# Spreading the norm sums and bias transposes among the modulation rows, and sharing the first scaling between VectorE and ScalarE

## The chip, the cores and the metric

The kernel runs on one NeuronCore of a Trainium2 chip. The metric is the device time of one execution in microseconds (us), lower is better; the figure for the kernel before is the median of three runs. Everything is float32.

## The reference, cut to what matters

The program computes two transformer blocks over 256 tokens of width 1024. The first is a conditioned block (attention of two kinds over 256 latent and 256 context tokens, then a mixture of 32 experts), the second has four mixers and a gated feed-forward. The change touches only the start of the first block:

```python
mod_lat = (jax.nn.silu(c) @ w_ada[l] + b_ada[l])[:, None, :]
mod_ctx = (jax.nn.silu(c_ctx) @ w_ada[l] + b_ada[l])[None, None, :]
sa, sca, ga, sf, scf, gf = jnp.split(mod_lat, 6, axis=-1)
...
def rmsnorm(x, w):
    xf = x.astype(jnp.float32)
    y = xf * lax.rsqrt(jnp.mean(xf * xf, axis=-1, keepdims=True) + EPS)
    return (y * w.astype(jnp.float32)).astype(x.dtype)

def modulate(h, shift, scale):
    return h * (1 + scale) + shift

l_dq, l_dk, ... = mixer_inputs(modulate(rmsnorm(x, attn_norm_w[l]), sa, sca), *mp, ang)
c_dq, c_dk, ... = mixer_inputs(modulate(rmsnorm(ctx, attn_norm_w[l]), csa, csca), *mp, None)
```

`mixer_inputs` multiplies these activations by `w_in` (the projections dq, dk, cq, ckv, kr, dv), rotates some of them (rope) and normalises others.

## The kernel before, in words

**Layout and order.** Activations are held transposed, features on the 128 partitions in 8 tiles k = 0 to 7, tokens along the free axis. `hT[:, k, 256:512]` holds tile k of the latent activations, `hT[:, k, 0:256]` that of the context. The order of the whole first part is one hand-written list, `PRE` (from L324): a list of steps, over which each engine loops by itself (`tensor_pre`, `vector_pre`, `scalar_pre`) and emits its own share of each step, so that a step's place in the list is its place in every engine's queue. GpSimd has its own program (`pool_pre`).

**The modulation row.** `w_ada` comes in 8 loads of 1 MB per third of it, one for each k. Step `("mrow", 0, k)` (L555) multiplies the padded silu of the two conditions by load k, in four column groups that accumulate in one PSUM bank. After the eighth, ScalarE copies the bank out (L830), `("mcol", 0)` transposes it with four matmuls (L562), VectorE adds the bias (L1025) and makes `aw = (1 + scale) * weight` in two instructions (L1035, L1037).

**The first norm.** ScalarE squares x (L867) into `hT[:, k, 0:256]`; steps `("xsum", 0)` and `("xsum", 4)` add the squares over the partitions by multiplying with ones (L581, four tiles each). ScalarE takes the root (L874), VectorE the reciprocal (L1028) and eight products `x * r` (L1032). Then `("h", 0)` multiplies each of the eight tiles by its column of `aw` and adds the shift, in place (L1043, eight VectorE instructions). Each raises `h_ready`, on which the matmuls of dq wait, tile by tile (L595).

**Bias transposes.** Steps `("b1t", 0..3)` transpose the experts' biases (L539), with a ScalarE copy each (L819); nothing needs them before the experts.

**The context.** `("ctxsquare",)` has ScalarE square the context (L854); `("rms", "ctx")` sums these (L588, after the second dq), and `("h", 1)` scales the context's tiles, VectorE first (L1047), ScalarE after (L879). From dk on the matmuls need both halves: they wait for `h_ready` of 8 + k + 1.

**Loads.** SyncE issues all big loads in one queue: x, the eight `w_ada` loads, then w_in for dq (two), the context, and the rest of w_in; a load into a slot waits until the matmuls that used the slot are done (L1782). The second third of `w_ada` is not multiplied by TensorE but added up by VectorE, `("add", k)` (L1019, L1016), beside the projections.

**GpSimd's tables.** `pool_pre` builds four tables one after the other by doubling (L759 to L767, from 4 elements a partition up to 512), writes each to DRAM with two DMAs (L773, L774) and waits for these before it starts the next (the memset at L749). The last instruction of a table raises `table_done`.

**The attention's start.** In `PRE`, after the projections, come two steps `score` (scores of one head and token tile; VectorE takes the maxima, L1098, ScalarE the exponentials, L924), then `("soft", 0, 0)` (VectorE, L1108 to L1117), qn, qr, a third score, and then qn, qr, kn (L633) and mv (L638), whose results ScalarE and VectorE move out of PSUM (qn at L901). VectorE's share of every `soft` begins with

```python
                elif kind == "soft":
                    w.wait_ge(table_done, 4)
```

Dense groups from there on rotate over four PSUM banks: the first kn (`("kn", 0)`) takes the bank of `("qn", 1)` and so waits for ScalarE's copy of that one, which stands in ScalarE's queue behind the exponentials of the third score, and these wait for VectorE's maxima, which stand behind `("soft", 0, 0)` in VectorE's queue.

After the attention come the output projection, the router, and the experts in the order of how many tokens they have; their weights (384 MB in all) stream in through SyncE's queue. The second block follows.

Of the kernel before, what the change touches and what calls it, by code (L numbers as in the profile page):

```python
# [5 lines left out]
ALU = mybir.AluOpType  # L6
ACT = mybir.ActivationFunctionType
# [170 lines left out]
def build(nc, I, out):  # L178
    ctx = ExitStack()
    with ctx:  # L180
# [3 lines left out]
        def sem(name):  # L184
            return ctx.enter_context(nc.semaphore(name))
# [20 lines left out]
        def Pm(name, i=None):  # L206
            a, b = PAR[name]
            return par[:, a:b] if i is None else par[:, a + i:a + i + 1]
# [32 lines left out]
        b1t = arena[:, TOP:AR]  # L241
# [3 lines left out]
        xv = xT[:, :].rearrange("p (k t) -> p k t", k=8)  # L245
# [6 lines left out]
        ctx_in, x_in, more_in = sem("ctx_in"), sem("x_in"), sem("more_of_cst_in")  # L252
        silu_e, c2_zero, c2_ready = sem("silu_e"), sem("c2_zero"), sem("c2_ready")
        sq_ready, sq_spent, rb_ready = sem("sq_ready"), sem("sq_spent"), sem("rb_ready")
        h_scaled, h_ready, rope_done, rope_kept = sem("h_scaled"), sem("h_ready"), sem("rope_done"), sem("rope_kept")
        norm_ready, lam_sem = sem("norm_ready"), sem("lam_ready")
        max_ready, p_ready = sem("max_ready"), sem("p_ready")
# [33 lines left out]
        rbs = take(2, 256)  # L291
        ctxT = take(8, 256)
        hT = take(8, 512)
# [15 lines left out]
        mods = sm(96).rearrange("p (j v) -> p j v", v=2)  # L309
        aw = sm(16).rearrange("p (j v) -> p j v", v=2)  # L310
# [11 lines left out]
        w_in = I["w_in"]  # L322

        PRE = [("silu",)] + [("phase", i) for i in range(8)] + [("power", k) for k in range(7)] + [("rms", "x")]  # L324
        PRE += [("mrow", 0, k) for k in range(4)] + [("xsum", 0), ("mrow", 0, 4), ("xsum", 4), ("mrow", 0, 5), ("b1t", 0), ("mrow", 0, 6), ("b1t", 1), ("mrow", 0, 7)]
        PRE += [("mcol", 0), ("b1t", 2), ("b1t", 3), ("aw",), ("h", 0), ("ctxsquare",)]
        late = []

        BESIDE = {("dk", j): [("add", j)] for j in range(4)}
# [43 lines left out]
        for i in range(len(UNITS) + 1):  # L373
# [10 lines left out]
            if i and i % 2 == 0:  # L384
                h = i // 2 - 1
# [28 lines left out]
        for s in PRE:  # L414
            kind = s[0]
            if kind == "mrow":
                m, k = s[1:]
# [7 lines left out]
            elif kind == "add":  # L425
                k = s[1]
# [94 lines left out]
        def tensor_pre(pe, w):  # L521
# [10 lines left out]
            for s in PRE:  # L532
                kind = s[0]
                if kind == "b1t":
# [3 lines left out]
                    for j in range(4):  # L538
                        i = pe.transpose(psum(s, j * 128, (j + 1) * 128)[0:32, :], b1col[:, :, s[1] * 4 + j], ident)  # L539
                    i.then_inc(pe_done, 1)  # L540
                elif kind == "mrow":
                    m, k = s[1:]
# [13 lines left out]
                elif kind == "mcol":  # L556
# [4 lines left out]
                    for j in range(4):  # L561
                        i = pe.transpose(psum(s, j * 128, (j + 1) * 128), rowb[m % 2][:, j * 128:(j + 1) * 128], ident)  # L562
                    i.then_inc(pe_done, 1)
                elif kind == "subroot":
                    room(G[s])
                    for h in range(4):
                        w.wait_ge(sub_square, h + 1)
                        i = pe.matmul(psum(s, 0, 256)[32 * h:32 * h + 32, :], ones[:, 0:32], sqh[h], start=True, stop=True, skip_group_check=True)
                    i.then_inc(pe_done, 1)
                elif kind == "subln":  # L570
                    h = s[1]
# [10 lines left out]
                elif kind == "rms" and s[1] != "x":  # L582
# [3 lines left out]
                    for k in range(K):  # L586
                        w.wait_ge(sq_ready, q + k + 1)
                        i = pe.matmul(psum(s, 0, n), ones, hT[:, k, 0:256] if s[1] == "ctx" else sqb[(q + k) % 2][:, 0:n], start=k == 0, stop=k == K - 1, skip_group_check=True)  # L588
                        i.then_inc(sq_spent, 1)
                elif kind in ("dq", "cq"):  # L590
                    j = s[1]
                    room(G[s])
                    for k in range(8):
                        w.wait_ge(h_ready, k + 1)
                        i = pe.matmul(psum(s, 0, 256), tile("w_" + kind, k, j * 128, (j + 1) * 128), hT[:, k, 256:512], start=k == 0, stop=k == 7, skip_group_check=True)  # L595
                    i.then_inc(pe_done, 1)
                elif kind in ("dk", "ckv"):
                    room(G[s])
                    key, a = ("w_dk", s[-1] * 128) if kind == "dk" else ("w_cq", 256)
                    for k in range(8):  # L600
                        w.wait_ge(h_ready, 8 + k + 1)
                        i = pe.matmul(psum(s), tile(key, k, a, a + 128), hT[:, k, :], start=k == 0, stop=k == 7, skip_group_check=True)
                    i.then_inc(pe_done, 1)
                elif kind == "kr":
                    room(G[s])
                    for k in range(8):
                        w.wait_ge(h_ready, 8 + k + 1)
                        for q in range(2):
                            i = pe.matmul(psum(s)[64 * q:64 * q + 64, :], tile("w_cq", k, 384, 448), hT[:, k, :], start=k == 0, stop=k == 7, skip_group_check=True)
                    i.then_inc(pe_done, 1)  # L610
# [6 lines left out]
                elif kind in ("qn", "qr"):  # L617
                    h = s[1]
# [10 lines left out]
                elif kind == "kn":  # L629
                    h = s[1]  # L630
# [19 lines left out]
                elif kind == "score":  # L650
                    _, h, t = s
# [25 lines left out]
                elif kind == "value":  # L677
                    h = s[1]
# [106 lines left out]
        def scalar_pre(act, w):  # L785
# [4 lines left out]
            for s in PRE:  # L790
# [64 lines left out]
                elif kind == "rms":  # L855
# [16 lines left out]
                    w.wait_ge(eps_set, 1)  # L872
                    w.wait_ge(sq_spent, q + K)
                    act.activation(rms_into(key), psum(s, 0, n), ACT.Sqrt, scale=1.0 / RMS_D[key], bias=eps).then_inc(moved[g.bank], 1)  # L874
                elif kind == "h" and s[1]:
                    w.wait_ge(moved[G["mcol", 0].bank], G["mcol", 0].use)
                    for k in range(8):
                        w.wait_ge(h_scaled, k + 1)
# [54 lines left out]
        def vector_pre(dve, w, own):  # L933
            dt, th, kk, wc, wsn, lbr, lbi, dn, t1, t2, t3, t4, t5 = phase_t
            are, aim = Pm("s5_are"), Pm("s5_aim")
            for s in PRE:
# [89 lines left out]
                elif kind == "rms":  # L1026
                    w.wait_ge(moved[g.bank], g.use)
                    dve.reciprocal(rms_into(s[1]), rms_into(s[1])).then_inc(rb_ready, 1)  # L1028
                    if s[1] == "x":
                        w.wait_ge(rb_ready, T["rb", "x"])  # L1030
                        for k in range(8):
                            own.count(dve.tensor_tensor(hT[:, k, 256:512], xv[:, k, :], rbs[:, 0, :], ALU.mult))  # L1032
                elif kind == "aw":
                    w.wait_ge(moved[G["mcol", 0].bank], G["mcol", 0].use)
                    own.count(dve.tensor_scalar(aw, mods[:, 8:16, :], 1.0, None, ALU.add))  # L1035
                    own.wait()
                    own.count(dve.tensor_tensor(aw, aw, Pm("attn_w").unsqueeze(2).to_broadcast([128, 8, 2]), ALU.mult))  # L1037
                    own.wait()
                elif kind == "h":
                    if s[1] == 0:  # L1040
                        own.wait()
                        for k in range(8):
                            dve.tensor_scalar(hT[:, k, 256:512], hT[:, k, 256:512], aw[:, k, 0:1], mods[:, k, 0:1], ALU.mult, ALU.add).then_inc(h_ready, 1)  # L1043
                        continue
                    w.wait_ge(rb_ready, T["rb", "ctx"])
# [2049 lines left out]
```

## Time and profile before

| | |
|---|---|
| median of three runs | 1820.44 us (1818.83 to 1822.33) |
| the profiled execution | 1820.19 us |
| its span in the trace | 1818.1 us |
| TensorE busy | 1654.9 us, 91% of the span |
| VectorE busy | 480.2 us, 26% |
| ScalarE busy | 263.0 us, 14% |
| GpSimd busy | 145.7 us, 8% |
| read from HBM | 540.33 MB |

Start times in the rows are microseconds from the start of the span. PE is TensorE's matmuls, DVE is VectorE, ACT ScalarE, POOL GpSimd. In a row of the timeline "[6.16 <-issue]" says how long the engine sat idle before the row and what ended that; PEclk is the granted clock of TensorE as a share of 2.4 GHz, so 0.50 is 1.2 GHz. A float32 matmul of the program shows up as two records.

### The profile page before, as it was taken

The page shows a single profiled execution, that of the slowest core. Times are in us where ns is not written, and L with a number is a line of the kernel's source. Part 1 is how long each engine was busy: PE and PEld are TensorE (multiplying, and loading weights), DVE is VectorE, ACT ScalarE, POOL GpSimd, SP SyncE. Part 2 cuts the span into 40 slices and gives each one's busy share as a digit, 9 for nine tenths or more (in the row PEclk, how much of TensorE's full clock was granted, in tenths as well). Part 3 has the DMA queues.
Part 4 walks back from the last instruction along what each step waited for, and adds up shares of the span by engine and source line. Part 5 has one row for each costly group of instructions (what it writes and reads, how often), then busy time and mean ns, then how long its engine had stood idle before and what let it go on. Part 6 is the DMA issues. An engine that isn't in the chain of part 4 may idle for free.

```text
span 1818.1 us, 19674 instructions
## 1 busy us (share of the span) xinstructions
PE 1654.9 (91%) x8178; PEld 1004.8 (55%) x8178; DVE 480.2 (26%) x1012; ACT 263.0 (14%) x554; POOL 145.7 (8%) x277
## 2 busy tenths in 40 slices
PE   5999999949997699948899996899999999999997
PEld 2644674414343154413344442377778888888886
DVE  5656421202121102202111220245576212211101
ACT  2114321101011011101011110023213100200000
POOL 6673000000000000000000000010002000000000
PEclk8999999979998799978999998999999999999998
DMA  9567478999999999999999999963452344534340
GB/s 375 204 234 263 168 306 349 428 419 424 425 426 428 426 428 424 424 428 427 421 427 426 427 427 427 419 242 120 158 180 99 134 144 162 209 118 160 139 162 24
DMA packets 93916, 546.95 MB, mean 301 GB/s; under 512 B 6539, under 2 KB 18455, under 8 KB 62844
## 3 DMA queue, kind: packets, MB, share of 16 engines
q1 hardware_dynamic: 88960, 529.82, 72.0%
q0 software_dynamic: 4128, 14.42, 2.2%
q8 instruction: 67, 1.10, 0.2%
q10 hardware_dynamic: 732, 1.38, 0.2%
q14 instruction: 29, 0.24, 0.0%
HBM read 540.33 MB, written 7.62 MB: 301 GB/s over the span
## 4 chain that ended last, share of the span: by engine, by line
PE 64%; DMA 20%; DVE 1%; SPq 1%; issue 0%; ACT 0%; DVEq 0%
PE PS L1408 16%; DMA arena<-in_w 11%; DMA ring<-in_w 9%; PE PS L2368 8%; PE PS L1433 8%; PE PS L2202 4%; PE PS L2394 4%; PE PS L2215 3%; PE PS L2223 3%; PE PS L1384 2%; PE PS L1444 2%; PE PS L2209 2%; PE PS L1418 2%; PE PS L2358 2%; PE PS L2231 2%; PE PS L2249 1%
## 5 line engine op out<-in xcount | busy, mean ns | idle before, releaser
L1408 PE MATMUL PS<-arena 128*64 128x512 f32 (+2 forms) x984 | 271.2, 651 | 60.1 <-DMA ring<-in_w 39.7
L1408 PE MATMUL PS<-ring,arena 128*64 128x512 f32 (+2 forms) x928 | 220.7, 636 | 41.8 <-DMA arena<-in_w 29.0
L1408 PEld LDWEIGHTS PS<-arena 128*64 128x64 f32 (+2 forms) x984 | 84.1, 139 | 201.1 <-issue 200.5
L1433 PE MATMUL PS<-ring,arena 128*64 128x512 f32 (+2 forms) x576 | 143.2, 628 | 11.4 <-DMA ring<-in_w 7.2
L2368 PE MATMUL PS<-arena,ring 128*128 128x256 f32 x704 | 152.5, 379 | 0.0
L1680 DVE TENSOR_SCALAR arena<-PS 128x512 f32<-128x512 f32 x28 | 19.4, 691 | 501.7 <-PE PS L1418 501.7
L1408 PEld LDWEIGHTS PS<-ring,arena 128*64 128x64 f32 (+2 forms) x928 | 67.1, 134 | 152.0 <-issue 151.5
L2368 PEld LDWEIGHTS PS<-arena,ring 128*128 128x128 f32 x704 | 133.6, 190 | 18.1
L1433 PE MATMUL PS<-arena 128*32 128x512 f32 (+2 forms) x392 | 96.1, 619 | 8.7 <-DMA ring<-in_w 5.0
L1433 PEld LDWEIGHTS PS<-ring,arena 128*64 128x64 f32 (+2 forms) x576 | 46.4, 138 | 88.1 <-issue 88.1
L2202 PE MATMUL PS<-arena,ring 128*128 128x256 f32 x384 | 85.0, 380 | 0.7 <-DVE arena L2673 0.7
L1545 ACT ACTIVATE arena<-arena 128x512 f32<-128x512 f32 x28 | 17.5, 630 | 424.2 <-DVE arena L1680 424.2
L2202 PEld LDWEIGHTS PS<-arena,ring 128*128 128x128 f32 x384 | 72.2, 190 | 11.7 <-issue 1.3
L2833 POOL DMA_DIRECT2D arena<-in_s_bre x1 | 0.6, 611 | 944.3 <-DVE xT L1714 944.3
L2394 PE MATMUL PS<-arena,ring 128*128 128x256 f32 x352 | 76.1, 379 | 0.0
L2394 PEld LDWEIGHTS PS<-arena,ring 128*128 128x128 f32 x352 | 66.9, 190 | 9.1
L1433 PEld LDWEIGHTS PS<-arena 128*32 128x32 f32 (+2 forms) x392 | 29.5, 128 | 60.0 <-issue 59.1
L1408 PE MATMUL PS<-cst,arena 128*32 128x512 f32 (+2 forms) x136 | 61.1, 592 | 0.0
L1384 PEld LDWEIGHTS PS<-arena 128*128 128x128 f32 x448 | 54.1, 196 | 10.0 <-issue 9.6
L2215 PE MATMUL PS<-arena,ring 128*128 128x256 f32 x256 | 58.4, 382 | 0.0
L1694 DVE COPY arena<-PS 128x512 f32<-128x512 f32 x14 | 9.7, 692 | 183.8 <-PE PS L1433 183.8
L2223 PE MATMUL PS<-arena,ring 128*128 128x256 f32 x256 | 58.0, 379 | 0.0
(479 smaller groups left out, 2051.5 us busy)
## 6 DMA issues: line engine op xcount, KB each, us to landing
ring<-in_w SPq DMA_DIRECT2D x92, 2048.0 KB, 22.1
arena<-in_w SPq DMA_DIRECT2D x74, 2048.0 KB, 22.9
ring<-in_w_ada SPq DMA_DIRECT2D x24, 1024.0 KB, 8.6
arena<-in_w SPq DMA_DIRECT2D x24, 1024.0 KB, 20.2
cst<-in_w SPq DMA_DIRECT2D x24, 1024.0 KB, 20.7
ring<-in_w_in SPq DMA_DIRECT2D x22, 1024.0 KB, 13.7
ring<-in_w_up SPq DMA_DIRECT2D x20, 1024.0 KB, 8.7
ring<-in_w_gate SPq DMA_DIRECT2D x16, 1024.0 KB, 7.0
```

What stands on the lines that cost most here:

```text
L1384: m = pe.matmul(bank(("gx", i, c), j * S, (j + 1) * S), of[:, j % 2, :], sel[:, t, :], start=t == 0, stop=t == 1, skip_group_check=True)
L1408: m = pe.matmul(bank(("up", i, b))[rows[n], :], xs[:, k, rows[n]], tiles[n][:, b * 512:(b + 1) * 512], start=k == 0, stop=False, skip_grou ...
L1418: m = pe.matmul(bank(("up", i, b))[rows[n], :], one.to_broadcast([128, width]), b1t[:, b * 512:(b + 1) * 512], start=False, stop=True, ski ...
L1433: m = pe.matmul(bank(("down", i, c))[rows[n], :], actT[:, k, rows[n]], tiles[n][:, a:a + 512], start=k == 0, stop=k == 7, skip_group_check ...
L1444: m = pe.matmul(bank(("y", i, c), q * 256, (q + 1) * 256), ysr[:, j * 128:(j + 1) * 128], pgt[i % 3], start=True, stop=True, skip_group_ch ...
L2202: i = pe.matmul(psum(s, q * 256, (q + 1) * 256), tile((name, j // 4), k, a, a + 128), xn[:, k, :], start=k == 0, stop=k == 7, skip_group_c ...
L2209: i = pe.matmul(psum(s, 0, m), xn[:, k, t * 128:(t + 1) * 128], tile((name, j), k, 0, m), start=k == 0, stop=k == 7, skip_group_check=True)
L2215: i = pe.matmul(psum(s, 0, 256), tile(("wgate", bi, f // 4), k, f % 4 * 128, f % 4 * 128 + 128), xn[:, k, :], start=k == 0, stop=k == 7, s ...
L2223: pe.matmul(psum(s, 0, 256), tile(("wgate", bi, f // 4), k, a, a + 128), xn[:, k, :], start=k == 0, stop=k == 7, skip_group_check=True)
L2231: i = pe.matmul(psum(s, 256, 512), tile(("wbr", bi, f // 4), k, a, a + 128), yt[:, k, :], start=k == 0, stop=k == K - 1, skip_group_check= ...
L2368: return pe.matmul(psum(("ff", f), half * 256, half * 256 + 256), tile((key, f // 4), k, a, a + 128), src[:, k, :], start=k == 0, stop=k = ...
L2394: i = pe.matmul(psum(("acc", j // 2), j % 2 * 256, j % 2 * 256 + 256), tile(("wd", c), k % 2, j * 128, (j + 1) * 128), hh[:, k, :], start= ...
```

## The change

It has three parts.

1. **The order of `PRE`.** The two xsum steps stand after the second and the third modulation row (they stood after the fourth and the fifth), and the four b1t steps after the fourth to the seventh row (they stood after the sixth and the seventh, and two of them behind `mcol`).
2. **The products `x * r`.** VectorE makes those of the even tiles first, then those of the odd ones; the odd ones raise a semaphore of their own, `x_scaled`.
3. **The step `("h", 0)`.** VectorE scales the four even tiles; ScalarE scales the four odd ones with an Identity activation whose scale and bias are columns of `aw` and of the modulation (raising `h_other`). The waits of dq, cq, dk, ckv and kr are renumbered to match. ScalarE's new share stands in its queue between the copies of the modulation row and the squares of the context.

```diff
         PRE = [("silu",)] + [("phase", i) for i in range(8)] + [("power", k) for k in range(7)] + [("rms", "x")]
-        PRE += [("mrow", 0, k) for k in range(4)] + [("xsum", 0), ("mrow", 0, 4), ("xsum", 4), ("mrow", 0, 5), ("b1t", 0), ("mrow", 0, 6), ("b1t", 1), ("mrow", 0, 7)]
-        PRE += [("mcol", 0), ("b1t", 2), ("b1t", 3), ("aw",), ("h", 0), ("ctxsquare",)]
+        PRE += [("mrow", 0, 0), ("mrow", 0, 1), ("xsum", 0), ("mrow", 0, 2), ("xsum", 4), ("mrow", 0, 3), ("b1t", 0), ("mrow", 0, 4), ("b1t", 1)]
+        PRE += [("mrow", 0, 5), ("b1t", 2), ("mrow", 0, 6), ("b1t", 3), ("mrow", 0, 7), ("mcol", 0), ("aw",), ("h", 0), ("ctxsquare",)]
...
                     for k in range(8):
-                        w.wait_ge(h_ready, k + 1)
+                        w.wait_ge(h_other if k % 2 else h_ready, k // 2 + 1)
                         i = pe.matmul(psum(s, 0, 256), tile("w_" + kind, k, j * 128, (j + 1) * 128), hT[:, k, 256:512], start=k == 0, stop=k == 7, skip_group_check=True)
...
-                        w.wait_ge(h_ready, 8 + k + 1)
+                        w.wait_ge(h_ready, 4 + k + 1)
...
-                elif kind == "h" and s[1]:
+                elif kind == "h" and not s[1]:
+                    w.wait_ge(aw_ready, 1)
+                    for k in range(1, 8, 2):
+                        w.wait_ge(x_scaled, k // 2 + 1)
+                        act.activation(hT[:, k, 256:512], hT[:, k, 256:512], ACT.Identity, scale=aw[:, k, 0:1], bias=mods[:, k, 0:1]).then_inc(h_other, 1)
+                elif kind == "h":
...
                         w.wait_ge(rb_ready, T["rb", "x"])
-                        for k in range(8):
-                            own.count(dve.tensor_tensor(hT[:, k, 256:512], xv[:, k, :], rbs[:, 0, :], ALU.mult))
+                        for k in (0, 2, 4, 6, 1, 3, 5, 7):
+                            i = dve.tensor_tensor(hT[:, k, 256:512], xv[:, k, :], rbs[:, 0, :], ALU.mult)
+                            if k % 2:
+                                i.then_inc(x_scaled, 1)
+                            else:
+                                own.count(i)
                 elif kind == "aw":
                     w.wait_ge(moved[G["mcol", 0].bank], G["mcol", 0].use)
                     own.count(dve.tensor_scalar(aw, mods[:, 8:16, :], 1.0, None, ALU.add))
                     own.wait()
-                    own.count(dve.tensor_tensor(aw, aw, Pm("attn_w").unsqueeze(2).to_broadcast([128, 8, 2]), ALU.mult))
-                    own.wait()
+                    dve.tensor_tensor(aw, aw, Pm("attn_w").unsqueeze(2).to_broadcast([128, 8, 2]), ALU.mult).then_inc(aw_ready, 1)
+                    w.wait_ge(aw_ready, 1)
                 elif kind == "h":
                     if s[1] == 0:
                         own.wait()
-                        for k in range(8):
+                        for k in range(0, 8, 2):
                             dve.tensor_scalar(hT[:, k, 256:512], hT[:, k, 256:512], aw[:, k, 0:1], mods[:, k, 0:1], ALU.mult, ALU.add).then_inc(h_ready, 1)
```

## Rows read from the trace of the kernel before

**Rows 1.** Stretches of 20 us: busy time of each engine, PEclk, DMA share, GB/s
```profile
300.00:320.00 20.00, 20.00 (x98) 7.15 (x96) 4.37 (x8) 3.93 (x7) 0.00 (x0) 1.00 0.64 254
320.00:340.00 20.00, 20.00 (x96) 6.74 (x94) 5.26 (x8) 1.26 (x2) 0.00 (x0) 1.00 1.01 429
```

**Rows 2.** The chain that ended last: start, length, what
```profile
347.48 23.34 DMA arena<-in_w
```

**Rows 3.** TensorE's timeline, 12 to 60 us: start, length, what
```profile
12.78 1.73 PE L555 MATMUL PS<-ring,arena 128*32 128x512 f32 x8 [0.46 <-DMA ring<-in_w_ada]
...
17.76 1.93 PE L555 MATMUL PS<-ring,arena 128*32 128x512 f32 x8 [1.42 <-DMA ring<-in_w_ada]
19.62 2.66 PE L581 MATMUL PS<-arena,cst 128*128 128x256 f32 x8
...
23.21 1.99 PE L581 MATMUL PS<-arena,cst 128*128 128x256 f32 x8
...
28.23 1.06 PE L555 MATMUL PS<-ring,arena 128*32 128x512 f32 x8
30.09 0.66 PE L562 MATMUL PS<-cst,arena 128*128 128x128 f32 x4 [0.80 <-ACT arena L830]
...
37.78 11.13 PE L595 MATMUL PS<-arena,ring 128*128 128x256 f32 x32 [6.16 <-issue]
...
52.19 7.07 PE L595 MATMUL PS<-arena,ring 128*128 128x256 f32 x32
```

**Rows 4.** Timeline of VectorE and ScalarE, 25 to 41 us
```profile
25.29 1.28 ACT L874 ACT_TABLE_LOAD   x1 [13.14 <-PE PS L581]
...
28.88 6.38 DVE L1032 TENSOR_TENSOR arena<-xT,arena 128x256 f32<-128x256 f32 x8
...
36.43 6.05 DVE L1043 TENSOR_SCALAR arena<-arena,small 128x256 f32<-128x256 f32 x8
...
38.23 2.56 ACT L854 ACTIVATE arena<-arena 128x256 f32<-128x256 f32 x8 [5.94 <-DMA arena<-in_ctxT]
```

**Rows 5.** Stretches of 1 us, columns as in rows 1
```profile
34.00:35.00 1.00, 0.00 (x0) 0.00 (x0) 1.00 (x2) 0.00 (x0) 1.00 (x2) 0.83 1.11 353
...
45.00:46.00 1.00, 1.00 (x7) 0.87 (x6) 0.10 (x1) 0.38 (x1) 0.00 (x0) 1.00 1.08 396
```

**Rows 6.** GpSimd's timeline: where the tables end (L773) and start (L749)
```profile
50.12 0.10 POOL L749 MEMSET arena<- 128x4 f32 x1 [7.44 <-DMA phase_scratch<-arena]
...
78.58 0.60 POOL L773 DMA_DIRECT2D phase_scratch<-arena  x1 [0.30 <-POOL arena L767]
...
86.18 0.10 POOL L749 MEMSET arena<- 128x4 f32 x1 [6.47 <-DMA phase_scratch<-arena]
...
119.40 0.60 POOL L773 DMA_DIRECT2D phase_scratch<-arena  x1 [0.30 <-POOL arena L767]
...
125.62 0.10 POOL L749 MEMSET arena<- 128x4 f32 x1 [5.09 <-DMA phase_scratch<-arena]
...
147.97 0.60 POOL L773 DMA_DIRECT2D phase_scratch<-arena  x1 [0.30 <-POOL arena L767]
```

**Rows 7.** Timelines of VectorE, ScalarE and TensorE, 149 to 158 us
```profile
149.02 0.15 DVE L1108 RECIPROCAL small<-small 128x1 f32<-128x1 f32 x1
...
152.78 0.65 ACT L901 ACTIVATE arena<-PS 128x256 f32<-128x256 f32 x2
...
153.80 3.60 PE L633 MATMUL PS<-arena,ring 128*128 128x512 f32 x8
```

**Rows 8.** VectorE's additions, and one table instruction of GpSimd beside and without one
```profile
69.16 3.12 DVE L1016 SCALAR_TENSOR_TENSOR ring<-ring,arena 128x2048 f32<-128x2048 f32 x1
...
106.60 5.43 DVE L1016 SCALAR_TENSOR_TENSOR ring<-ring,arena 128x2048 f32<-128x2048 f32 x2
...
70.09 3.08 POOL L760 TENSOR_TENSOR arena<-arena 128x512 f32<-128x512 f32 x1
...
141.82 1.04 POOL L760 TENSOR_TENSOR arena<-arena 128x512 f32<-128x512 f32 x1
```

More of the change, by code:

```diff
@@ L254, in build @@
         sq_ready, sq_spent, rb_ready = sem("sq_ready"), sem("sq_spent"), sem("rb_ready")
+        aw_ready, h_other, x_scaled = sem("aw_ready"), sem("h_other"), sem("x_scaled")
         h_scaled, h_ready, rope_done, rope_kept = sem("h_scaled"), sem("h_ready"), sem("rope_done"), sem("rope_kept")
@@ L606, in tensor_pre @@
                     for k in range(8):
-                        w.wait_ge(h_ready, 8 + k + 1)
+                        w.wait_ge(h_ready, 4 + k + 1)
                         for q in range(2):
```

## The prediction

> **What bounds the kernel now.** I first read the busy time by stretches, to see whether the start of the program matters to its end. Up to 320 us TensorE is busy all the time while the DMA engines have room (0.64 of their time between 300 and 320 us), and from 320 us on they are full [rows 1]; the chain that ended last turns from TensorE to the experts' loads at 347 us [rows 2]. Those loads start when TensorE frees their space, so what TensorE gains before 320 us, and keeps, comes out at the end one for one; what is regained before that point is worth nothing. Next I read TensorE's timeline of the first 60 us, where it still has holes. The modulation rows run as their loads land (each waits for a DMA); the eighth runs at 28.23, and its transposes end at 30.75 [rows 3]. Then TensorE waits for the first scaled tile until 37.78, and the 32 records of the first two dq take 11.13 us where the next 32 take 7.07 [rows 3]. VectorE's timeline says why: root at 25.29, reciprocal, eight products up to 35.26, then the modulation's bias and `aw`, which were ready to be made since 30.8, then eight scalings from 36.43 to 42.48 [rows 4]. The clock is the second reason: granted full until TensorE had been idle for about 3 us, it falls in the stretch at 34 us and is back at 45 us [rows 5]. Last I followed the path forward from there for a wait that doesn't move with TensorE, and found GpSimd's: its fourth table ends 0.30 us before the DMA at 147.97, at 147.67 [rows 6], and the first soft step, which needs it, starts at 149.02 [rows 7]. That is 1.35 us of slack.
>
> **The front, step by step.** The loads of `w_ada` are not moved, so row eight stays at 28.23 and the transposes at 30.09 to 30.75 [rows 3]. The two b1t steps that stood behind them lie elsewhere now, in waits for loads: nothing gained or lost. The first xsum can start at the end of row two, 12.78 + 1.73 = 14.5; with two xsum steps of 2.66 and 1.99 us and a row between them of 1.06 to 1.93 us the second one ends between 20.2 and 21.1 (before: 25.2) [rows 3]. From there root and table load take 1.80 us (25.29 to the reciprocal at 27.09), the reciprocal 1.79 (to 28.88) and the products 6.38 [rows 4]; so they end at about 30.6 instead of 35.26. The transposes are done at 30.75, so the chain over the norm and the chain over the modulation now end together. From the end of the products to the first scaling it was 36.43 - 35.26 = 1.17 us [rows 4], so scaling starts at 31.9. VectorE's four take 4 x 0.76 = 3.0 us (6.05 / 8 each) [rows 4]; ScalarE's four, by the context's squares of the same size, 4 x 0.32 = 1.3 us (2.56 / 8) [rows 4], beside them. For a scale that is a column, the trace has no ScalarE row on this tile; the bound above is VectorE's 0.76, which would change nothing, since each engine then still keeps the other's pace. The first tile is there at 32.7 and the last at 34.9, instead of 37.2 and 42.5.
>
> At the full clock dq 0 is done 0.44 us behind the last tile (7.07 / 16 for a tile's two records), at 35.4, and dq 1 3.5 us later, at 38.9. At the half clock throughout it would be 32.7 + 14.1 = 46.8. TensorE is idle for only 2 us (30.75 to 32.7), but lightly loaded since 29, and before it kept the full clock for about 3 us of idleness [rows 3, 5]; I take a fall for part of the time, and 41 for the end of dq 1 (39 to 44). The context then has to be there: its squares can't start before 38.23, when its load lands, and take 2.56 us [rows 4], so it costs nothing unless the clock stays full. The sums over the context follow in 3.5 us, and the third dq starts at 44.5 instead of 52.19 [rows 3]: 7.7 us earlier, between 5 and 9.5.
>
> ScalarE's new share stands ahead of the context's squares, and ends at about 33.5 while these wait for a load until 38.23: free, with 4.7 us of cover. The later w_in loads, the additions and the ropes follow TensorE or land ahead of their use. The cst load moves a little; nothing waits for it.
>
> **What becomes of it.** GpSimd's tables hang on its own queue and its own DMAs [rows 6]; they don't move with TensorE. TensorE reaches `("kn", 0)` at 153.80 - 7.7 = 146.1, but that needs the bank of `("qn", 1)`, whose copy ended 4.14 us after soft began (152.78 + 0.38 against 149.02) [rows 7]; and soft can't begin before the table at 147.67 + 0.05. So kn 0 starts at 147.7 + 4.25 = 151.95 at the earliest: of the 7.7 us 1.85 are left (the slack of 1.35, and 0.5 that TensorE had over ScalarE's copy), and TensorE stands still for some 6 us instead.
>
> The table's own end moves, though. A VectorE addition over 2048 elements with two operands in SBUF stops GpSimd for its length: L760 took 3.08 us beside one and 1.04 without [rows 8], 2.0 us lost. The seven of them run between 69.16 and 112.0 [rows 8]; tables two and three took 28.5 and 33.2 us (50.12 to 78.58, 86.18 to 119.40), the fourth, alone, 22.35 [rows 6]. That is 6.1 and 10.9 us over. One of the seven fell at the end of table two and into the DMA wait behind it (78.58 to 86.18), where it cost nothing. The additions now come 5 to 8 us earlier and the tables at most 1; one more of the additions may fall into that wait (2 us gained), the eight products of the context's scaling fall before table two (some 0.9 gained), or the one that was free falls inside table two (2 us lost). I take the fourth table 2 us earlier, with the ends -4 and +2. kn 0 then starts at 149.95, 3.85 us earlier than before.
>
> **The clock at the new stall.** TensorE comes back after some 4 us of idleness, longer than the 3 us after which it had lost its clock at 34 us; from 37.78 it took until 45 to have it again [rows 3, 5]. At half clock for 4 us, half of the work done in them is lost: 2 us (0 if the clock holds, 3.5 if it takes the 7.2 us of before). The Trainium skill (TensorE: Matmul & The Clock Gate, The HAM clock gate) says that an idle stretch puts the array back to 1.2 GHz and that the phase of this gate is not tied to the kernel's start, so that the loss differs from run to run; by that rule the full loss would come in some runs and none in others. The trace agrees as far as one execution can: 0.83 in the stretch at 34 us, behind 2.4 us of idleness [rows 3, 5].
>
> **Sum.** 1820.19 - 1.85 - 2 + 2 = 1818.3 for an execution like the profiled one, which stands 0.25 us under the median of the runs. I predict 1818.3, a gain of some 2 us. The measurement tells about 0.2% (3.6 us) from no change, so this counts as within it.
>
> **Rivals.**
> (A) The tables end earlier still, or the clock holds: 1.85 + 2 to 4, with a loss of 0 to 1, so 4 to 6 us: 1815.2. For it: how many additions fall into the DMA waits is a matter of 2 us each. Against it: a stall over 3 us speaks for a fallen clock. 0.25.
> (B) The gain of the front comes through whole: 1820.2 - 7.7 = 1812.5. It would need the soft step not to wait for the table, or the tables to follow TensorE; the wait stands in the code, and the rows show 1.35 us of slack. 0.04.
> (C) Slower: the additions, moved against the tables, all cost their 2 us, so the fourth table ends 2 us or more later (past 149.5, from where no gain is left: 1.85 - 2), and the clock falls at the stall and takes 7 us to return: 1.85 - 2 - 3.5 = -3.65 and beyond: 1824. For it: only one addition of seven had been free. Against: the context's products leave table two. The Trainium skill (SBUF — State Buffer, Who interferes with whom) has the side that starts second blocked for the other's whole instruction; with the row's 3.12 us instead of my 2.0 for the lost time this rival would be at 1825. 0.08.
> (D) The front gives little, because the clock is low through both dq (third dq at 50.3, 1.9 us earlier): then the table hardly binds, TensorE doesn't stall, and 1818.3 to 1820 comes out as well. 0.10.
>
> **Numbers.** The forecast (table binds, clock falls) has 0.53 and gives 1816.7 to 1820.5. The range, 1814.2 to 1822.5, takes in A and D, half of the clock's and the table's bad ends, and the spread of runs (1.8 us to either side). Faster by over 0.2%: most of A, B, and a tail of the forecast, 0.31. Slower: C, 0.08. The rest, 0.61.
>
> **What would show it.** The products L1032 should start at about 24 and end by 31; four L1043 from about 32, four ScalarE scalings beside them; the third dq at 44 to 46. A wait of VectorE of several us on GpSimd ahead of L1108, about 146 us; a hole of 3 to 6 us on TensorE before L633, and half clock behind it. If the third dq is 7 us earlier and L633 is too, the table is not what I take it for; if L633 starts later than 152, the tables moved the wrong way; if the first dq starts after 35, the front is wrong.

## The result, and the profile after

The change made the kernel slower: 1824.72 us (median of 20 runs, 1822.18 to 1827.91) against 1820.82 (20 runs, 1818.13 to 1825.61), ratio 1.0019 with a 95% interval of 1.0012 to 1.0026. The forecast was 1818.3, no measurable change, with 1814.2 to 1822.5 as its range; the time lies 2.2 us above the range. In time it is rival (C), slower at 1824, that came; its two effects show below (a table that ends later, a clock that falls), but not the cause that it gave for the table. The profiled execution took 1827.03 us, at the slow end of its runs, with a span of 1824.9.

TensorE's timeline of the changed kernel, lines that answer to [rows 3]:

```profile
14.73 2.68 PE L582 MATMUL PS<-arena,cst 128*128 128x256 f32 x8
...
18.33 1.99 PE L582 MATMUL PS<-arena,cst 128*128 128x256 f32 x8
...
28.05 1.06 PE L556 MATMUL PS<-ring,arena 128*32 128x512 f32 x8 [0.88 <-DMA ring<-in_w_ada]
29.91 0.65 PE L563 MATMUL PS<-cst,arena 128*128 128x128 f32 x4 [0.80 <-ACT arena L831]
32.33 8.83 PE L596 MATMUL PS<-arena,ring 128*128 128x256 f32 x32 [1.77 <-DVE arena L1053]
...
44.45 7.07 PE L596 MATMUL PS<-arena,ring 128*128 128x256 f32 x32
```

VectorE and ScalarE, answering to [rows 4]:

```profile
24.00 3.48 DVE L1038 TENSOR_TENSOR arena<-xT,arena 128x256 f32<-128x256 f32 x8
...
31.53 2.81 DVE L1053 TENSOR_SCALAR arena<-arena,small 128x256 f32<-128x256 f32 x4
...
31.52 2.07 ACT L880 ACTIVATE arena<-arena,small 128x256 f32<-128x256 f32 x4 [1.67 <-DVE small L1047]
```

The front does what it was meant to: the last row and its transposes stay where they were, the first dq starts at 32.33 instead of 37.78, and the third at 44.45 instead of 52.19, 7.7 us earlier.

Then the attention's start, first VectorE, then TensorE, answering to [rows 7]; VectorE's timeline:

```profile
149.88 0.16 DVE L1118 RECIPROCAL small<-small 128x1 f32<-128x1 f32 x1 [9.14 <-POOL arena L768]
```

TensorE's:

```profile
154.14 6.33 PE L634 MATMUL PS<-arena,ring 128*128 128x512 f32 x8 [8.04 <-issue]
160.31 3.60 PE L639 MATMUL PS<-ring,arena 128*128 128x512 f32 x8
```

Stretches of 4 us, columns as in [rows 1]:

```profile
146.00:150.00 4.00, 0.09 (x1) 0.00 (x0) 0.12 (x1) 0.00 (x0) 3.69 (x4) 0.91 0.73 240
150.00:154.00 4.00, 0.00 (x0) 0.00 (x0) 3.82 (x11) 1.68 (x6) 3.65 (x5) 0.50 0.72 256
```

VectorE waits 9.14 us for the fourth table; TensorE stands still for 8.04 us and comes back at 1.2 GHz, so that kn's eight records take 6.33 us instead of 3.60. mv starts at 160.31, 3.08 us later than before, and so does the router (its first transposes, at 252.57 before):

```profile
255.65 1.94 PE L1352 MATMUL PS<-cst,xT 128*128 128x128 f32 x16
```

So 3.1 us of the 6.8 between the two spans arise ahead of the router. The rest lies behind it, in the part whose length varies by more than that between traces (below).

GpSimd's tables, answering to [rows 6]:

```profile
119.11 0.60 POOL L774 DMA_DIRECT2D phase_scratch<-arena  x1 [0.30 <-POOL arena L768]
...
127.79 0.10 POOL L750 MEMSET arena<- 128x4 f32 x1 [7.55 <-DMA phase_scratch<-arena]
...
150.15 0.60 POOL L774 DMA_DIRECT2D phase_scratch<-arena  x1 [0.30 <-POOL arena L768]
```

The third table's end stands where it stood (119.11 against 119.40), but its write took longer, 7.55 us of waiting against 5.09, and the fourth table ends at 149.85 instead of 147.67.

### The profile page after: what moved, and what is told of

Same layout as the page of the kernel before. It is cut to its first block, busy times and chain, and to the rows that moved or that the text cites. A ratio compares the mean times of both kernels' runs of the same rounds, so it can differ in the third digit from the quotient of the medians.

```text
span 1824.9 us, 19675 instructions
## 1 busy us (share of the span) xinstructions
PE 1656.2 (91%) x8178; PEld 1007.9 (55%) x8178; DVE 471.3 (26%) x1008; ACT 264.8 (15%) x558; POOL 145.1 (8%) x277
## 4 chain that ended last, share of the span: by engine, by line
PE 62%; DMA 21%; DVE 1%; SPq 1%; issue 0%; ACT 0%; DVEq 0%
DMA ring<-in_w 16%; PE PS L1418 15%; PE PS L2378 8%; PE PS L1443 8%; DMA arena<-in_w 5%; PE PS L2212 4%; PE PS L2404 4%; PE PS L2225 3%; PE PS L2233 3%; PE PS L1394 2%; PE PS L1454 2%; PE PS L2219 2%; PE PS L2241 2%; PE PS L2368 2%; PE PS L1428 2%; PE PS L2259 1%
## 6 DMA issues: line engine op xcount, KB each, us to landing
ring<-in_w_in SPq DMA_DIRECT2D x22, 1024.0 KB, 13.6
```

## The experiments

Ratios are to the kernel before, run beside each version. "The router" stands for the start of its first transposes (L1342 before), "the third dq" for the start of the second group of 32 records of L595. In the first trace of the kernel before, the router is at 252.57; in three later traces of it and of versions that leave its front alone, it is at 250.72 to 250.80 (see the second traces below).

**The wait taken out, after and before.** The later `value` step waits for the tables' DMAs in any case.

```diff
                 elif kind == "soft":
-                    w.wait_ge(table_done, 4)
```

> The changed kernel, whose soft steps no longer wait for GpSimd's fourth table (the first value step still waits for the tables' DMAs, as before). Theory (the change gains 7.7 us at the front, the wait for the table takes all of it and the half clock behind the stall takes more): the first kn starts at 146 us instead of 154.1, at full clock; the router's first transposes start at 245 us, 7.7 us before the 252.6 of the kernel before; time about 7.5 us below before (1813), about 11 below the changed kernel. Rival 1 (the loss arises elsewhere, for instance in the stream of the experts' weights): the first kn moves but the time stays within 2 us of before. Rival 2 (another wait stands right behind the table): the first kn starts at 150 or later.

> The kernel before, with the same wait taken out. Theory: TensorE was not held by the table there (slack of 1.35 us at soft, 0.5 at the copy), so kn stays at 153.8 and the time within 1 us of before. If the wait cost something by itself, whatever the front does, this one gains too: by the rival that the wait is a plain loss in both kernels, 3 us or more.

Measured: the changed kernel without the wait 1815.18 us, ratio 0.9970 (0.9959 to 0.9981); the kernel before without it 1821.43, ratio 1.0006 (0.9997 to 1.0014). The wait costs the kernel before nothing, and the changed one 9.5 us (its median less this one, from two series of runs). TensorE's timeline in the changed kernel without the wait:

```profile
147.54 3.67 PE L634 MATMUL PS<-arena,ring 128*128 128x512 f32 x8 [0.79 <-issue]
...
247.24 1.95 PE L1351 MATMUL PS<-cst,xT 128*128 128x128 f32 x16
```

VectorE's, one of the soft step's instructions:

```profile
142.28 1.62 DVE L1122 SCALAR_TENSOR_TENSOR arena<-arena,small 128x512 f32<-128x512 f32 x1
```

The stall is gone but for 0.79 us, the clock stays full, and the router starts 5.3 us before the kernel before in its first trace, 3.5 before its usual 250.7. I had expected 146 and 245: of the 1.5 us missing at kn 0.65 are the front (third dq at 45.10 instead of 44.45), and most of the rest is VectorE, whose soft instructions now run beside GpSimd's table, this one for 1.62 us where it took 0.75. Rival 1 (the loss arises in the experts' stream) and rival 2 (another wait right behind) both fall.

**The fourth table cut short.** The wait stays, seven of the last table's eight doublings are left out, so that this table is not the right one.

```diff
-                for k in range(8):
+                for k in range(7, 8) if q == 3 else range(8):
                     n = 1 << k
```

> The changed kernel whose fourth table does only its last doubling (seven of eight left out, so that table's values are not computed and the second block's last scan group is not the reference's); the wait stays. The table ends some 15 us earlier, at about 134.5 us. Theory: what counts is only when the fourth table ends, so this gives what taking the wait out gives: first kn at 146 us, router at 245, time about 7.5 us below before. If it is 2 us or more slower than the version without the wait, the wait has a cost beyond the table's end; if faster, VectorE and GpSimd hindering each other has a price when the wait is gone.

Measured 1813.79 us, ratio 0.9966 (0.9953 to 0.9979). The table ends at 132.55, kn starts at 144.71, the router at 243.48. With the wait in place and the table early the whole gain is there, so it is the time at which the table ends that costs, and nothing else about the wait.

**The stall filled.** The last qn is computed seven times.

```diff
-                    for k in range(2):
+                    for k in [0, 1] * (7 if s == ("qn", 3) else 1):
```

> The changed kernel with the last qn's four matmuls done seven times over (same result), which fills some 6 us of TensorE's stall in front of the first kn. Theory: the table still holds kn to about 154 us, but the granted clock stays at 2.4 GHz, so kn's eight records take 3.6 us instead of 6.3 and everything behind is 2.7 us earlier than in the changed kernel: time 2.5 to 3 us below it, about 1 us above before. Rival (the clock costs nothing, it is hidden behind VectorE and ScalarE at that place): the router starts where it does in the changed kernel and the time is the same.

Measured 1821.27 us, ratio 1.0003 (0.9995 to 1.0012). TensorE, the two lines that answer to those of the changed kernel, and the router:

```profile
154.00 3.67 PE L634 MATMUL PS<-arena,ring 128*128 128x512 f32 x8 [1.53 <-issue]
157.50 3.60 PE L639 MATMUL PS<-ring,arena 128*128 128x512 f32 x8
...
252.84 1.95 PE L1352 MATMUL PS<-cst,xT 128*128 128x128 f32 x16
```

kn starts within 0.14 us of where it does in the changed kernel, but at the full clock, and the router starts 2.8 us earlier. From kn to the router it is 98.84 us here, 98.77 in both traces of the kernel before, and 101.51 and 101.29 in the two of the changed kernel. So the clock's share, measured by itself, is 2.5 to 2.7 us; the medians differ by 3.4 us. Useless work in the hole brings the changed kernel back to the time of the kernel before.

**Tables in two places.** GpSimd builds them by turns in the space of qn and qr and in the old one; ScalarE's copies of qn and VectorE's rope of qr wait for the third table's write.

```diff
-        Cw, Sw = mix[:, 0:4, :], mix[:, 4:8, :]
+        TABLES = [(qn, qr), (mix[:, 0:4, :], mix[:, 4:8, :])]
...
-                if q:
-                    w.wait_ge(tabs_out[q - 1], 32)
+                Cw, Sw = TABLES[q % 2]
+                if q > 1:
+                    w.wait_ge(tabs_out[q - 2], 32)
```

> The changed kernel with the wait kept, and GpSimd's tables built in two places by turns (the space of qn and qr, free until the attention, and the old one), so that a table waits only for the write of the one before the last. Theory: the three gaps of 8 to 9 us between tables shrink to the issue of two DMAs (1.3 us), the fourth table ends near 128 us instead of 149.9, the wait no longer binds, and the first kn comes at 144.7 to 147 at full clock: time 6 to 8 us below before, like the version with a short fourth table, but with everything computed. Rival (tables packed closer hinder VectorE, or VectorE them, and the front or the additions fall behind): third dq later than 47, or the fourth table past 140, and time no better than 3 us below before.

> The kernel before with the same two places for the tables. Theory: the table did not bind there, so nothing is gained: within 1.5 us of before. If it gains 3 us or more, the tables cost the kernel before something other than the wait at soft.

Measured: on the changed kernel 1813.41 us, ratio 0.9967 (0.9955 to 0.9980); on the kernel before 1820.99, ratio 1.0005 (0.9994 to 1.0016). GpSimd's timeline in the first of these:

```profile
107.24 0.60 POOL L775 DMA_DIRECT2D phase_scratch<-arena  x1 [0.30 <-POOL arena L769]
...
108.36 0.12 POOL L751 MEMSET arena<- 128x4 f32 x1
...
131.68 0.60 POOL L775 DMA_DIRECT2D phase_scratch<-arena  x1 [0.30 <-POOL arena L769]
```

And TensorE's:

```profile
146.25 3.60 PE L634 MATMUL PS<-arena,ring 128*128 128x512 f32 x8
...
245.02 1.95 PE L1356 MATMUL PS<-cst,xT 128*128 128x128 f32 x16
```

The last table starts 1.1 us behind the DMA issue of the third and ends at 131.38 (I had expected 128), and kn starts without a stall. So this version computes everything and beats both kernels: the one before by 6.7 us and the changed one, whose median comes from another series of runs, by 11. The same edit is worth nothing without the change.

**The parts of the change.** The new order alone (with the wait, and twice without), and the shared scaling alone:

> The kernel before with the new order of the steps alone (xsum and b1t among the rows), all eight first scalings on VectorE, and soft's wait for the table taken out, so that a gain of the front can be seen in the time. Theory: VectorE's products end by 28, scaling starts at 31.5 and takes 6 us at the pace of 0.76 each; dq 0 ends at about 38 instead of 45, the third dq starts at 45 to 47 instead of 52.2: most of the front's 7.7 us is the order's. Time 4 to 6 us below before. Rival (the share is what counts, since a tile every 0.76 us keeps TensorE at half clock): third dq at 49 or later, time within 3 us of before.

> The new order alone without the wait, once more, since its time came out only 0.6 us below before while its trace had the router 4.2 us earlier. If the part behind the router is what varies from run to run (the stream of the experts' weights), the time comes out 2 to 5 us below before this time or in both together, and the trace shows the router at 248 to 250; if it is again within 1 us of before with the router at 248, something behind the router takes the gain back.

> The kernel before with the shared scaling alone (order as before), and soft's wait taken out. Theory: scaling still starts at 36.4, the last tile is there at 39.5 instead of 42.5, the clock is low from 34 to 45 as before, so only 1 to 3 us are gained: third dq at 49 to 51, time 1 to 3 us below before. Rival (the share is what counts): third dq at 47 or earlier.

> The kernel before with the new order alone, the wait for the table kept. Theory: third dq at about 46.4, then the same stall as in the changed kernel, 1 to 2 us shorter; kn at the table's end plus 4.2 us and at half clock; router at 252 to 256, time 1 to 4 us above before. Rival (VectorE's scaling of all eight tiles leaves the clock alone and the stall is too short for it): time at or below before.

| without the wait | median, us | ratio (95%) | third dq | router |
|---|---|---|---|---|
| new order | 1819.51 | 0.9994 (0.9984 to 1.0003) | 46.39 | 248.38 |
| new order, again | 1818.03 | 0.9984 (0.9973 to 0.9994) | 46.23 | 248.20 |
| shared scaling | 1820.39 | 1.0002 (0.9992 to 1.0012) | 47.70 | 249.65 |

At the front, against two traces of the kernel before (52.19 and, below, 50.42), these traces make the order worth 4 to 6 us and the share 3 to 4.5; the two together, over all six traces with both, are worth 5 to 9 (third dq between 43.10 and 45.64). In the trace with the wait kept (48.70, below) the order is worth only 1.7 to 3.5 us. The share came out earlier than I expected (49 to 51), because scaling started at 34.34 there instead of 36.43 and the clock came back at 40 instead of 45. The first of these is no merit of the share: in the later traces of the kernel before and of its versions, scaling starts at 33.5 to 34.3 too.

I had expected the order to gain 4 to 6 us of time and the share 1 to 3. Against the usual router of the kernel before (250.7) the order brings the router forward by 2.4 us and the share by 1.1, and the times (0.6 and 3.5 us below before for the order, 0.3 above for the share) don't contradict that. The part behind the router's start varies too, by up to 4.9 us between traces: span less router is 1564.9 us in the version of before without the wait, 1569.8 in the second of the order without it, 1565.5 and 1566.6 in the two of before and 1569.2 in both of the changed kernel. One trace can't tell how much of 2 us arrives at the end, and 11 runs can hardly. What sets this part's length stays open: it is the stream of the experts' weights, in which no edit was tried.

The order alone, with the wait kept, is the most telling. Its median is 1825.41 us, ratio 1.0030 (1.0017 to 1.0042), but the profiled execution took 1817.7 while the other seven took 1824.02 to 1828.03. In that execution TensorE shows this:

```profile
48.70 7.07 PE L595 MATMUL PS<-arena,ring 128*128 128x256 f32 x32
```

And at the first kn:

```profile
150.40 3.60 PE L633 MATMUL PS<-arena,ring 128*128 128x512 f32 x8
```

And GpSimd behind the fourth table:

```profile
144.56 0.60 POOL L773 DMA_DIRECT2D phase_scratch<-arena  x1 [0.30 <-POOL arena L767]
```

The third dq starts 2.3 us later than in the same order without the wait (46.39), and the table ends at 144.26, the earliest of all traces with the tables as they were. So kn could have started at about 148.5, TensorE reaches it only at 150.40, without a stall and at full clock, and the run is the fastest of the eight, 6.3 us or more ahead of the rest. The early table did most of it. By an estimate from these traces, with this table and the front at 46.4 the stall would have been 0.4 us (148.5 less 150.4 - 2.3), while with this front and a table at 147 to 150 it would have been 1 to 4 us. The stall and the half clock that I had expected here, with the router at 252 to 256, did not show in the trace (249.17). Of the seven others there is no trace; that they stalled is inferred from their times.

**Second traces.**

> The changed kernel once more, for a second trace of it. Theory: the third dq at 43 to 46, the fourth table's end between 148 and 152, the first kn 4.2 us behind that, preceded by a stall of 6 us or more, and half clock behind it; router between 253.5 and 257. If the fourth table ends before 147.7 this time, the 2 us by which it came later than before in the first trace are chance, and only the clock is left as the reason why the changed kernel is slower rather than equal.

> The kernel before once more, for a second trace. Theory: the third dq between 50 and 52.5 (by how long TensorE's clock stays low), the fourth table's end between 145.5 and 148.5, kn without a stall over 1 us, router between 250.5 and 253. A stall in front of kn of 2 us or more would say that the table binds before the change too.

The changed kernel gave 1824.12 us, ratio 1.0015 (1.0005 to 1.0026), the kernel before 1820.48, ratio 0.9998 (0.9988 to 1.0007), so the slowdown was measured twice. TensorE in the changed kernel's second trace:

```profile
151.32 6.11 PE L634 MATMUL PS<-arena,ring 128*128 128x512 f32 x8 [6.58 <-issue]
157.27 3.60 PE L639 MATMUL PS<-ring,arena 128*128 128x512 f32 x8
...
252.61 1.95 PE L1352 MATMUL PS<-cst,xT 128*128 128x128 f32 x16
```

GpSimd there, the start of its fourth table and the write behind it:

```profile
124.98 0.10 POOL L750 MEMSET arena<- 128x4 f32 x1 [3.81 <-DMA phase_scratch<-arena]
...
147.33 0.60 POOL L774 DMA_DIRECT2D phase_scratch<-arena  x1 [0.30 <-POOL arena L768]
```

TensorE in the second trace of the kernel before:

```profile
50.42 7.07 PE L595 MATMUL PS<-arena,ring 128*128 128x256 f32 x32
```

Further on in the same trace:

```profile
151.95 3.60 PE L633 MATMUL PS<-arena,ring 128*128 128x512 f32 x8
...
250.72 1.94 PE L1342 MATMUL PS<-cst,xT 128*128 128x128 f32 x16
```

This time the changed kernel's fourth table ends at 147.03, earlier than the 148 to 152 that I had expected and 0.6 us earlier than in the first trace of before, and the stall and the half clock are there all the same. My condition for calling the later table chance was met. The other traces speak against chance, though. The fourth table starts at 124.98 to 127.79 in the five traces of the changed kernel and its versions (two places left aside), 126.6 in the mean, and at 123.75 to 125.62 in three of the kernel before and its version without the wait, 124.4 in the mean: 2.2 us later, with a small overlap.

The kernel before, on the other hand, turns out to vary by itself: its third dq starts at 50.42 here, and at 50.46 and 50.49 in its versions without the wait and with two places. The 52.19 on which I predicted was the late one of four. What sets it apart is TensorE's clock, in this stretch of the first trace (columns as in [rows 1]):

```profile
18.00:19.00 1.00, 1.00 (x8) 0.00 (x0) 0.00 (x0) 0.00 (x0) 0.80 (x6) 0.50 1.00 418
```

The granted clock is 0.50 from about 17.6 to 21 us there, and 1.00 over this whole time in the three others. The sums of squares end later, the root starts at 25.29 instead of 23.94 to 24.40, the products run later beside longer GpSimd instructions (6.38 us instead of 5.24 to 5.44), and scaling starts at 36.43 instead of 33.5 to 34.3.

## Why the prediction was wrong

**The front was right.** 7.7 us were forecast between the first traces and 7.7 measured; over six traces the changed front has its third dq at 43.10 to 45.64, around the forecast of 44.5. One term was off and cost nothing: the products took 3.48 us instead of 6.38. They ran beside GpSimd instructions of 32 to 128 elements (0.35 to 0.50 us each) where they had run beside such of 256 and 512 (0.67 to 1.22). But the norm was no longer what scaling waits for, as VectorE was idle for 3.13 us in front of the modulation's bias. dq 1 ended at 41.2 where I had taken 41.

**The chain behind it was right.** "of the 7.7 us 1.85 are left": the soft step at the table's end plus 0.03, kn 4.26 us behind it (4.25 in the forecast), TensorE at a standstill, half clock behind. Removing the wait, shortening the table and moving the tables forward each gave the gain back, and neither of the two edits that were also tried on the kernel before (the first and the last) changed its time.

**The step that failed is the table's end**, "I take the fourth table 2 us earlier". It ended 2.2 us later in one trace and 0.6 earlier in the other, against the late trace of before, and 4.1 and 1.2 us later against the second (145.80). In the first traces 1.85 - 2.2 = -0.35 remained instead of 3.85 us, and kn started 0.34 us later than before. I had counted only VectorE's additions, and taken the gaps between the tables, in which GpSimd waits for its own writes, as fixed.

- Tables two and three together took 60.9 us in the first trace of the changed kernel (29.11 and 31.81) and 61.7 in that of before (28.46 and 33.22). So the additions went my way, but by 0.8 us and not by 2; over all traces of both fronts it is 0.5 us in the mean (60.9 to 61.8 against 61.4 to 62.4).
- The two gaps behind them, from the issue of a table's write to the start of the next table, are where the time went. Together they took 16.5 and 13.6 us in the two traces of the changed kernel and 14.3 to 15.7 in its versions, against 13.8 and 12.3 in the two of before and 11.4 in its version without the wait: 2.6 us more in the mean. In the first trace it was the gap in front of table four (8.68 against 6.22), in the other four of the changed front the one in front of table three (8.6 to 9.8 against 6.1 to 7.6).

What lengthens a gap was not tested. Each holds two writes of 512 KB, beside the loads of SyncE's queue, and the change moves those loads against the tables; but the traced run of the order alone had 9.7 us in both gaps together, so the earlier front doesn't lengthen them every time. The bounds that I gave to the table (4 us early to 2 us late) came from the wrong cause and leaned the wrong way, and so did the reason of rival (C).

**The clock's term was too small.** I took 2 us for the half clock, with 0 to 3.5 as its bounds. kn's records lost 2.73 us in the first trace (6.33 - 3.60) and 2.51 in the second (6.11 - 3.60), and filling the hole returned as much. In the prediction I took from the Trainium skill (TensorE: Matmul & The Clock Gate, The HAM clock gate) that the loss would come in some runs only. What it says of an idle stretch, that the array is back at 1.2 GHz behind it, agrees with both traces (granted clock 0.50 behind standstills of 8.04 and 6.58 us); a run that stalls and loses nothing is not among them. At the front, where TensorE was idle for only 1.8 us, the clock does vary: from 32.3 the 32 records of two dq took 8.83 us in one trace and 7.50 in the other. I had also written that the clock was full until the hole at 31.6; in the trace that I read it was low from 17.6 to 21 as well.

**And the reference point.** The sum was made against one execution whose front was 1.7 us later than in three other traces of the same front. Its slack was no different: in the second trace of before the table ends at 145.80, so kn could have started at about 150.1, and it starts at 151.95, 1.85 us later again. In that execution TensorE and the table are both 1.9 us earlier, the table mostly by its gaps (1.5 us); whether these follow the loads that TensorE releases or vary by chance, no run tells. But the usual kn of the kernel before is at 151.95 to 152.03, not at the 153.80 that I counted from. kn of the changed kernel started at 154.14 and 151.32, in the mean 152.7, 0.8 later than usual, and 2.6 us of clock make 3.4; the medians differ by 3.9 in the first comparison and by 2.6 in the second. The chain of waits was right; the table's end was wrong in its cause and its sign, the clock's term was too small, and the reference was a late one.

## What to carry to other kernels

Before a front is made faster, follow the path from it to the next wait on an engine that runs by its own schedule, and take the slack there from several executions, with the gaps in which that engine waits for its own transfers: if the slack is smaller than the gain, the rest turns into a stall, and on TensorE the stall has a price of its own. An improvement that ends in such a wait can be worse than none: the pair of edits (front and table) gains 7 us, where the front alone loses 4 and the table alone gains nothing. A run far below its kernel's median is worth reading: here the order alone was fastest when the table, which it doesn't touch, was early.

## What the hardware showed beside that

TensorE's granted clock fell at about 33.2 us in the first trace of the changed kernel, although TensorE had been idle for only 0.80 and 1.77 us around 0.65 us of transposes, and it was back by 36.6. In the second trace, with the same gaps to 0.01 us, it didn't fall. The stretch of 1 us in which it fell:

```profile
33.00:34.00 1.00, 1.00 (x5) 0.81 (x4) 1.00 (x2) 0.60 (x2) 0.92 (x2) 0.60 1.08 357
```

A VectorE instruction on a single element a partition with two operands in SBUF (L1119 of the changed kernel without the wait) took 0.57 and 0.84 us beside GpSimd's 512-element instructions and 0.22 without them. So small instructions can be held up by GpSimd's long ones too.
